# Latent attention's scores from fp32r halves: five passes a unit in place of two fp32 products

## The reference, cut to what matters

```python
def chunk_causal_mla_attention(q_nope, q_pe, k_nope, k_pe, v):
    scale = (QK_NOPE + QK_ROPE) ** -0.5            # 128 and 64
    def one_block(args):                           # blocks of 128 queries
        qn_b, qp_b, i = args
        s = (jnp.einsum('bqhd,bkhd->bhqk', qn_b, k_nope)
             + jnp.einsum('bqhd,bkd->bhqk', qp_b, k_pe)) * scale
        q_idx = i * Q_BLOCK + jnp.arange(Q_BLOCK)
        s = jnp.where(chunk_mask(q_idx, k_idx)[None, None], s, jnp.finfo(jnp.float32).min)
        p = jax.nn.softmax(s, axis=-1).astype(v.dtype)
        return jnp.einsum('bhqk,bkhd->bqhd', p, v)
```

## Time and profile before

| What | Value |
|---|---|
| Median of three runs | 1967.65 us |
| The profiled execution's own time | 1970.33 us |
| Its span in the trace | 1968.6 us |
| PE busy | 1947.7 us, 99% of the span |
| DVE busy | 1419.8 us, 72% |
| ACT busy | 833.0 us, 42% |
| POOL busy | 92.2 us, 5% |
| Granted TensorE clock, mean | 0.997 |

### The profile page before, as it was taken

How to read it: one execution, slowest core, us unless ns; L and a number is a source line. 1 busy time by engine, 2 the same in 40 slices (tenths; PEclk the granted TensorE clock), 3 DMA queues, 4 the chain that set the end, 5 groups by cost and what they waited for, 6 DMA issues and landing times.

```text
span 1968.6 us, 24358 instructions
## 1 busy us (share of the span) xinstructions
PE 1947.7 (99%) x9737; PEld 1622.2 (82%) x9737; DVE 1419.8 (72%) x1989; ACT 833.0 (42%) x1305; POOL 92.2 (5%) x127
## 2 busy tenths in 40 slices
PE   9999999999999999999999999999999999999998
PEld 7887777888888888888888899988877788888886
DVE  6665687468656565836477888887898668887787
ACT  4454464335333333533323444444464445444343
POOL 1001240000000000000000010000022000000000
PEclk9999999999999999999999999999999999999999
DMA  5322212212332323233223323322133032332311
GB/s 176 107 87 65 90 61 86 86 43 91 102 107 86 107 86 107 86 107 104 89 86 104 116 87 110 119 93 86 55 80 107 22 103 79 121 115 86 107 65 65
DMA packets 139825, 181.12 MB, mean 92 GB/s; under 512 B 9792, under 2 KB 98496, under 8 KB 139712
## 3 DMA queue, kind: packets, MB, share of 16 engines
q1 hardware_dynamic: 137824, 178.04, 27.7%
q10 hardware_dynamic: 1632, 1.51, 0.2%
q0 software_dynamic: 256, 0.02, 0.0%
HBM read 177.44 MB, written 2.10 MB: 91 GB/s over the span
## 4 chain that ended last, share of the span: by engine, by line
PE 93%; DVE 4%; ACT 1%; issue 1%; DMA 0%; POOL 0%; SPq 0%; ACTq 0%; DVEq 0%; POOLq 0%
PE bank L690 20%; PE bank L692 20%; PE bank L691 20%; PE bank L1232 5%; PE bank L1231 5%; PE bank L1230 5%; PE bank L854 4%; PE bank L733 2%; PE bank L735 2%; PE bank L734 2%; PE bank L846 2%; PE bank L944 1%; PE bank L932 1%; PE bank L1159 1%; DVE w_lo L1362 1%
## 5 line engine op out<-in xcount | busy, mean ns | idle before, releaser
L690 PE MATMUL bank<-h_hi,w_hi 128*128 128x512 f32 x1384 | 546.5, 395 | 1.9 <-DVE w_lo L1362 0.9
L692 PE MATMUL bank<-h_hi,w_lo 128*128 128x512 f32 x1384 | 539.9, 390 | 0.0
L691 PE MATMUL bank<-h_lo,w_hi 128*128 128x512 f32 x1384 | 539.7, 390 | 0.0
L2266 ACT ACTIVATE w_hi<-raw 128x1024 fp32r<-128x1024 f32 (+2 forms) x207 | 203.1, 1020 | 275.6 <-PE bank L692 221.9
L690 PEld LDWEIGHTS bank<-h_hi,w_hi 128*128 128x128 f32 x1384 | 260.3, 188 | 59.2 <-issue 3.9
L692 PEld LDWEIGHTS bank<-h_hi,w_lo 128*128 128x128 f32 x1384 | 260.0, 188 | 54.5
L691 PEld LDWEIGHTS bank<-h_lo,w_hi 128*128 128x128 f32 x1384 | 260.3, 188 | 54.0 <-issue 1.9
L1362 DVE TENSOR_TENSOR w_lo<-raw,w_hi 128x1024 fp32r<-128x1024 f32 (+2 forms) x194 | 232.1, 1228 | 34.0 <-ACT w_hi L2266 33.3
L690 PE MATMUL bank<-g_hi,w_hi 128*128 128x512 f32 (+1 forms) x460 | 178.1, 387 | 1.3 <-issue 0.7
L692 PE MATMUL bank<-g_hi,w_lo 128*128 128x512 f32 (+1 forms) x460 | 172.9, 376 | 0.0
L691 PE MATMUL bank<-g_lo,w_hi 128*128 128x512 f32 (+1 forms) x460 | 172.5, 375 | 0.0
(11 more groups left out here) (287 smaller groups left out, 3153.9 us busy)
## 6 DMA issues: line engine op xcount, KB each, us to landing
raw<-w SPq DMA_DIRECT2D x32, 1024.0 KB, 5.3
arena<-w SPq DMA_DIRECT2D x32, 1024.0 KB, 5.0
raw<-w_up SPq DMA_DIRECT2D x22, 1024.0 KB, 5.1
raw<-a_w_in SPq DMA_DIRECT2D x16, 1024.0 KB, 5.3
raw<-w_in SPq DMA_DIRECT2D x11, 1024.0 KB, 5.4
raw<-w_down SPq DMA_DIRECT2D x11, 1024.0 KB, 5.0
raw<-w_mkv SPq DMA_DIRECT2D x8, 1024.0 KB, 5.3
raw<-a_w_out SPq DMA_DIRECT2D x8, 1024.0 KB, 5.0
```

Of the source, the lines that this page charges most:

```text
L690: nc.tensor.matmul(dst, a_hi, b_hi, start=(k == 0), stop=False)
L691: nc.tensor.matmul(dst, a_hi, b_lo, start=False, stop=False)
L692: last = nc.tensor.matmul(dst, a_lo, b_hi, start=False, stop=(k == n - 1))
L2266: A(hi, src, ACT.Copy).then_inc(w_hi_done, 1)
```

## The change

Scores of latent attention are now five fp32r passes. For the 128 plain features: hi by hi, hi by lo, lo by hi, from halves of each head's queries and keys. For the 64 rotary features, whose three passes would fill only half the array's rows, two passes of 128 rows do: one with the low and the high half of the queries stacked against the high keys twice (`low_high_rows` by `both_rows`), one with the high half and the mask rows against the low keys and the mask's key rows (`high_mask_rows` by `key_rows`).

The halves need places and makers. ACT makes the highs: six copies of 64 rows before the attention, then four copies a head (`high_of_head`: 128x512 twice, 64x512 twice). Head 0's are made during the key/value tiles, those of head h+1 in the first two steps of head h (`beside_mla`). POOL makes the lows: two for the shared rows, then three a head (`low_of_head`), and it starts a head only when all four highs of it are there. Before the first unit of each head PE waits for the head's three lows (`mla_low`). The places are parts of `h_hi`, `h_lo`, `g_hi` and `g_lo`, two sets in turn.

Besides, the two DVE copies of mask rows go, DVE waits once for `mla_high` before it takes the first value tile, and ACT's and DVE's pieces of the second output chunk move from steps 4 to 7 to steps 13 to 16 (`MLA_PIECES`). The key/value tiles keep their order on PE.

```diff
-        MEM_PIECES, MLA_PIECES = (2, 3, 14, 15, 18, 19), (5, 6, 22, 23, 30, 31)
+        MEM_PIECES, MLA_PIECES = (2, 3, 14, 15, 18, 19), (14, 15, 22, 23, 30, 31)
+        def head_halves(h):
+            if h % 2 == 0:
+                return (h_hi[:, 0, :], h_lo[:, 0, :]), (h_hi[:, 1, :], h_lo[:, 1, :])
+            if h < 4:
+                return (g_hi[:, 2, :], g_lo[:, 2, :]), (g_hi[:, 3, :], g_lo[:, 3, :])
+            return (h_hi[:, 3, :], h_lo[:, 3, :]), (h_hi[:, 4, :], h_lo[:, 4, :])
...
+            def low_of_head(h):
+                (q_hi, q_lo), (k_hi, k_lo) = head_halves(h)
+                rows = own_rows(h)
+                pool.wait_ge(mla_high, 6 + 4 * h + 4)
+                pool.wait_ge(mla_low, 2 + 3 * h)
+                for n, (lo, src, hi) in enumerate(((q_lo, mla_q[:, h, :], q_hi), (k_lo, mla_k[:, h, :], k_hi),
+                                                   (low_high_rows[h % 2][rows, :], mla_qr[rows, h, :],
+                                                    high_mask_rows[h % 2][rows, :]))):
+                    if n == 2:
+                        pool.wait_ge(mla_low, 2 + 3 * h + 2)
+                    G.tensor_tensor(lo, src, hi.bitcast(F32), ALU.subtract).then_inc(mla_low, 1)
...
+            for h in range(1, MLA_HEADS):
+                low_of_head(h)
...
             def mla_scores(h, i, dst):
-                n = P * (i + 1)
-                return several([(dst, mla_q[:, h, P * i:P * i + P], mla_k[:, h, 0:n], True, False),
-                                (dst, mla_qr[:, h, P * i:P * i + P], rope_k[h % 2][:, 0:n], False, True)])
+                n, block = P * (i + 1), slice(P * i, P * i + P)
+                if i == 0:
+                    pe.wait_ge(mla_low, 2 + 3 * (h + 1))
+                    if h == 4:
+                        pe.wait_ge(tile_taken, kv_end)
+                (q_hi, q_lo), (k_hi, k_lo) = head_halves(h)
+                return several([(dst, q_hi[:, block], k_hi[:, 0:n], True, False),
+                                (dst, q_hi[:, block], k_lo[:, 0:n], False, False),
+                                (dst, q_lo[:, block], k_hi[:, 0:n], False, False),
+                                (dst, low_high_rows[h % 2][:, block], both_rows[:, 0:n], False, False),
+                                (dst, high_mask_rows[h % 2][:, block], key_rows[h % 2][:, 0:n], False, True)])
...
-                    if c == 0 and h % 2:
-                        j = h // 2
-                        rows = slice(64 - 64 * j, 128 - 64 * j)
-                        dve.wait_ge(mla_masked, 8)
-                        keep_order(V.tensor_copy(mla_qr.rearrange("p (a j) n -> p j a n", j=2)[rows, j, :, :],
-                                                 q_rows[rows, :].rearrange("p (a n) -> p a n", a=1).to_broadcast([64, 4, S])))
...
+            for j in range(8):
+                if j == 4:
+                    dve.wait_ge(mla_high, 6)
+                take_kv(0, j)
...
+            def high_of_head(h, part):
+                (q_hi, _), (k_hi, _) = head_halves(h)
+                if part == 0:
+                    act.wait_ge(tile_taken, keys_start + h % 4 + 1 + 8 * (h // 4))
+                    high_of_mla(q_hi, mla_q[:, h, :])
+                    high_of_mla(k_hi, mla_k[:, h, :])
+                else:
+                    high_of_mla(high_mask_rows[h % 2][own_rows(h), :], mla_qr[own_rows(h), h, :])
+                    high_of_mla(low_high_rows[h % 2][other_rows(h), :], mla_qr[own_rows(h), h, :])
...
+            def beside_mla(s):
+                if s % 4 < 2 and s // 4 + 1 < MLA_HEADS:
+                    high_of_head(s // 4 + 1, s % 4)
+                if s + 1 in MLA_PIECES:
+                    split_high(1)
```

More of the change, by code:

```diff
@@ L195, in build @@
         f_z, f_a = at(12800, S), at(13312, S)
-        rstd_kv = at(17408, S)
         mix_rs = row_stats[:, 0:4]
@@ L254, in build @@
         mla_masked = sem("mla_masked")
+        mla_high = sem("mla_high")
+        mla_low = sem("mla_low")
         w_loaded = [sem("w_loaded0"), sem("w_loaded1")]
@@ L332, in build, with own_rows, other_rows @@
         GROUP = {"fox": HEADS, "sb": HEADS, "mem": 2, "mla": TT}
+        def head_halves(h):
[4 more added lines that the diff above has]
+            return (h_hi[:, 3, :], h_lo[:, 3, :]), (h_hi[:, 4, :], h_lo[:, 4, :])
+        def own_rows(h):
+            return slice(ROPE * (h % 2), ROPE * (h % 2) + ROPE)
+        def other_rows(h):
+            return own_rows(h + 1)
         LAG = 3
@@ L649, in _ @@
                 chunk_rows(n)
-            for c in range(NOT_SHARED, len(CHUNKS)):
+            def low_of_head(h):
[9 more added lines that the diff above has]
+                    G.tensor_tensor(lo, src, hi.bitcast(F32), ALU.subtract).then_inc(mla_low, 1)
+            for c in range(NOT_SHARED, len(CHUNKS)):
+                if c == NOT_SHARED + 10:
+                    pool.wait_ge(mla_high, 6)
+                    pool.wait_ge(w_split_pool, by_pool(c))
+                    for h in range(2):
+                        rows = own_rows(h)
+                        G.tensor_tensor(key_rows[h][rows, :], rope_k[h][rows, :], both_rows[rows, :].bitcast(F32), ALU.subtract)\
+                         .then_inc(mla_low, 1)
+                    low_of_head(0)
                 if SHARED[c]:
@@ L653, in _ @@
                     pool.wait_ge(w_hi_done, highs(c) + 2)
+                    if c == NOT_SHARED + 10:
+                        pool.wait_ge(mla_low, 5)
                     G.tensor_tensor(lo, src, hi.bitcast(F32), ALU.subtract).then_inc(w_split_pool, 1)
+            pool.wait_ge(w_split_pool, by_pool(len(CHUNKS)))
+            for h in range(1, MLA_HEADS):
+                low_of_head(h)
+            pool.wait_ge(mla_low, 2 + 3 * MLA_HEADS)
             pool.wait_ge(gain_loaded, 16)
@@ L1305, in _, with kv_tile @@
             h_n.n += 2
[L1306 to L1315, removed]
+            def kv_tile(j):
+                if j == 0:
+                    wait_chunk()
+                dst = next_bank()
+                if j < 4:
+                    full(split_sum(dst[:], w_tiles(2, slice(256 * j, 256 * j + P), rows_view), h_tiles(2, 3)))
+                else:
+                    t, slot = j - 4, slot_of(chunk.n)
+                    vals = [tuple(rows_view(w, slot)[:, k, :].rearrange("p (h n) -> p h n", n=256)[:, :, P:256]
+                                  for w in (w_hi, w_lo)) for k in range(2)]
@@ L1316, in _ @@
                     full(split_sum(dst[:].rearrange("p (h n) -> p h n", n=P),
                                    h_tiles(2, 3, slice(P * t, P * t + P)), vals))
-                chunk.n += 1
-            def mla_scores(h, i, dst):
-                n = P * (i + 1)
-                return several([(dst, mla_q[:, h, P * i:P * i + P], mla_k[:, h, 0:n], True, False),
-                                (dst, mla_qr[:, h, P * i:P * i + P], rope_k[h % 2][:, 0:n], False, True)])
+                if j == 7:
+                    chunk.n += 1
@@ new lines, in _ @@
+            for c in range(2):
+                for j in range(8):
+                    kv_tile(j)
+            kv_end = tile.n
+            def mla_scores(h, i, dst):
+                n, block = P * (i + 1), slice(P * i, P * i + P)
[9 more added lines that the diff above has]
+                                (dst, high_mask_rows[h % 2][:, block], key_rows[h % 2][:, 0:n], False, True)])
@@ L1327, in mla_values @@
                                  pt[:, P * k:P * k + P], k == 0, k == i) for k in range(i + 1)])
-            attention("mla", UNITS, mla_scores, mla_values,
-                      lambda s: back((s - 13) // 8, [(s - 13) % 8]) if s >= 13 else None, v_tiles=4)
+            def beside_mla(s):
+                if s >= 13:
+                    back((s - 13) // 8, [(s - 13) % 8])
+            attention("mla", UNITS, mla_scores, mla_values, beside_mla, v_tiles=4)
             back(2, [7])
@@ L2169, in _, with take_kv @@
             dve.wait_ge(rows_ready, 5)
[L2170 to L2174, removed]
-                    if c == 0 and h % 2:
-                        j = h // 2
-                        rows = slice(64 - 64 * j, 128 - 64 * j)
-                        dve.wait_ge(mla_masked, 8)
-                        keep_order(V.tensor_copy(mla_qr.rearrange("p (a j) n -> p j a n", j=2)[rows, j, :, :],
-                                                 q_rows[rows, :].rearrange("p (a n) -> p a n", a=1).to_broadcast([64, 4, S])))
[L2181 to L2186, removed]
+            settle()
+            def take_kv(c, j):
+                if j < 4:
+                    take(scaled(mla_k[:, 4 * c + j, :], rstd_kv))
+                else:
+                    take(lambda b: V.tensor_scalar(mla_v[:, j - 4, 512 * c:512 * c + 512], b[:],
+                                                   rstd_col[:, 4 + j:5 + j], None, ALU.mult))
+            for j in range(8):
+                if j == 4:
+                    dve.wait_ge(mla_high, 6)
```

(24 more changed lines are left out.)

5 lines of the change are left out of this document (4 added, 1 removed).

## The result

The changed kernel takes 1971.35 us in the median of 20 runs (1967.99 to 1976.45), the kernel before 1967.6 us in 20 runs beside it (1966.41 to 1968.84). The ratio is 1.0019, with a 95% interval of 1.0013 to 1.0025: slower by 3.75 us. The time lies inside the range of 1961.5 to 1972, but the forecast was no change, 1967.3, and its 0.17 for slower was put, all but 0.03, on two mechanisms that the profile doesn't bear out. So it was wrong by 4 us, and the cause is the subject here.

What follows compares the result with a forecast made beforehand. PE was taken to bound the kernel. Being 5.5 us behind at head 3, plus 0.3, less 5.8 saved later and 0.3 of short stops, gave -0.3 us: median 1967.3, range 1961.5 to 1972.

Steps and rivals of the forecast that it cites:

- two mechanisms: Narrow fp32r passes at 0.22 us (1971.7, chance 0.12); POOL and DVE colliding over SBUF ports (1971.3, chance 0.13).
- The passes: Latent attention scores: five fp32r passes replace fp32, 3.15 us a head after 4.3, saving 9.2 us over eight heads.
- The copies and head 0's halves: Key/value tiles: removing the DVE mask copies gains 0.5 us; making head 0's halves there costs nothing.
- POOL's subtraction: Each head's three lows on POOL: 1.29 us for each subtraction of 512 columns.
- the first loop: From head 0's scores to head 1's in latent attention: 8.8 us, where it was 4.9.
- Rival 4: POOL and DVE collide as fully as SBUF ports allow: 1971.3 us, or 1973 if PE is delayed; chance 0.13.
- The added wait: PE waits for the next head's lows: 9.5 us a head against 6.5 of work, some 3 us stopped.
- Net -0.3 us: Whole change: losses up to head 3, later savings and fewer short stops nearly cancel, leaving 0.3 us gained.
- After head 3: From step 13 `back` fills PE and hides the wait; heads 3 to 7 save 5.8 us.
- my signs of being wrong: Stops under 1.5 us each, stops also before heads 4 to 7, or narrow passes 0.2 us apart.
- slow pass that follows a stop: Key/value tiles: PE's 0.35 us stop counted as 0.5 with the slow pass behind it, an estimate.
- Rivals 2 and 4: Wait mostly hidden, 1962 us, or 1958 if wholly (chance 0.2); full POOL and DVE collision, 1971.3 us (chance 0.13).

Runs made afterwards that it cites:

- The run with head 0's halves: The changed kernel with all heads scoring from head 0's halves, other heads' highs, lows and waits left out; 1957.2 us, ratio 0.9946.
- the filled kernel: The changed kernel with useless fp32 products of ones on PE ahead of the waits before heads 1, 2 and 3; 1967.36 us, ratio 0.9996.

## Why the prediction was wrong

- **The passes** (9.2 us, with 0.11 for a narrow one): right. The run with head 0's halves gives 10.4 with the key/value part.
- **The copies and head 0's halves** (0.5): from the spread matmul to head 0 it is 23.14 us in place of 23.95, 0.8 less. Near enough. PE didn't wait for the halves.
- **POOL's subtraction** (1.29) and **the first loop** (8.8): 1.26 to 1.30, and 8.66. Right. Three lows end 3.94 us after the first begins, and three times 1.3 is 3.9, so no collision is to be seen there; before head 3 it may be 0.2 us (the low of 1.47). Rival 4 isn't what happened. Head 0's lows did meet DVE beside the key/value tiles: DVE's subtraction at 1500.97 took 2.17 us in place of 1.23, and POOL's pair at 1502.36 took 3.18 in place of 2.5 to 2.6. PE waited for neither.
- **The added wait**, "9.5 us a head", "PE stops some 3 us a head", "Net -0.3 us": this is the step that failed. A stop was priced at its own length, and what follows it at full clock. The loop itself was right: with the clock held up it is 9.2 us, and the filled kernel is 5.0 us behind at head 3 (1543.98 - 1493.21 = 50.77, less 45.77) against 5.5 forecast, and gains 6.2 afterwards against 5.8. Its 1967.36 is near my 1967.3, in part by luck: its stage is 1.2 us shorter than before (134.23 against 135.47), where I forecast 0.3. At half clock the loops grew to 10.4 and 10.8 and head 3's units lost part of their gain. The three stretches lack 0.16 x 10.43 + 0.16 x 10.77 + 0.14 x 11.78 = 5.0 us of full clock; 3.6 of it shows in the stage (137.85 against the filled kernel's 134.23). The rest probably lies where PE would have waited anyway; no run shows that by itself. The medians say 4.0.
- **After head 3** the waits vanish, as forecast: none before heads 4 to 7. Of my signs of being wrong none came up: the narrow passes 0.22 us apart are those at half clock, and at full clock they are 0.11.
- **The rivals** asked for a cheaper or dearer loop, or a dearer pass. None asked what a stop does to the work behind it. I wrote of a "slow pass that follows a stop" for a stop of 0.35 us and left it there, though the earlier trace rows and the granted clock of the earlier trace rows were in hand: before, PE was never idle for more than 0.4 us in this stage, so none of its rows could show the fall, and that was the reason to keep it as a rival with a price. Outside the stage the same trace did show it: the stop of 2.10 us at 235.84, with 0.86 behind it. I looked only at the stage. Rivals 2 and 4 also have a slip: they count four loops, but by the prediction's own account only three end in a stop, so they come to 1962.8 and 1970.3 in place of 1962 and 1971.3.

The Trainium skill ("TensorE: Matmul & The Clock Gate", Part 1: The HAM clock gate) has the two levels, and says that how many slow matmuls there are varies from run to run. By that, the trace agrees: stops of 2.07 and 2.09 us, one without a slow stretch and one with; one and the same stop of 2.10 us with some 3 us of slow work in four traces and some 7 in eight; and the changed kernel's runs scatter over 8.5 us where before's scatter over 2.4. It also says that the price is under 1% of a typical span. It is 0.2% here, and that decided the sign.

## What to carry to other kernels

A new wait on a busy TensorE costs its own length, and of the stops of 2.07 us and more in this kernel all but one brought the clock down, which took 1.7 or 3.4 us of full clock each; the stages grew by about a microsecond per stop beyond its own length. So read the granted clock by stretch on both sides of every stop, over the whole span of the kernel before too: one such stop far from the stage that you change shows the price. Where work of equal length can't be put into the stop, start the operands' makers a head earlier: moving the same instructions ahead turned 3.75 us lost into 9.0 gained. And a range that holds the time for the wrong reason is no support: filling the stop, which adds work and takes no wait away, told the two causes apart in one run.

## What the runs showed of the hardware that was not expected

- The clock fell at stops of 2.09, 2.10 (in all twelve traces), 2.41 (in two), 2.42, 2.72, 3.94 and 4.06 us, not at one of 2.07, and not at those of 1.38, 0.50 and 0.20. The fall came between the last microsecond or so of the stop and 1.4 us after work had begun again (the kernel before, 235.84).
- Over the changed kernel's 20 runs the time goes roughly with the mean granted clock: 1967.99 us at 0.997, 1969.44 at 0.996, four of 1972.99 to 1973.38 at 0.993, 1976.45 at 0.992. The 13 between, 1970.45 to 1972.12, have 0.994 to 0.996 in no clear order.
- In the first unit the first fp32r pass of 128 columns starts its follower after 0.06 us (1516.36, 1516.42), half of the 0.11 of those behind it.
- GpSimd's subtraction and ScalarE's copy take no less time for 64 partitions than for 128: 1.26 against 1.25 to 1.30 us, and 0.63 against 0.57.
